# One-hot products of the expert gates: rounded operands in two passes, and one-hots built four tokens at a time

## What is computed

```python
best_s, best_c = lax.top_k(cand_s.reshape(T, PEER_HEADS, K * K), K)
expert_id = jnp.take_along_axis(cand_id.reshape(T, PEER_HEADS, K * K), best_c, axis=-1)
gate = jax.nn.softmax(best_s, axis=-1)
...
u = expert_down[ib]
a = jnp.einsum('pd,ped->pe', xb, u).astype(jnp.float32)
act = jax.nn.gelu(a, approximate=False) * gb
v = expert_up[ib]
return jnp.einsum('pe,ped->pd', act.astype(xb.dtype), v)
```

## Time and profile before

| what | value |
|---|---|
| median of 3 runs | 1441.38 us (1441.08 to 1443.99) |
| the profiled execution | 1449.68 us |
| its span | 1447.7 us |
| TensorE matmuls busy | 1318.6 us, 91% |
| VectorE busy | 984.3 us, 68% |
| ScalarE busy | 663.0 us, 46% |
| GpSimd busy | 288.2 us, 20% |
| mean granted TensorE clock | 0.954 |

### The profile page before, as it was taken

One profiled execution on the slowest core, in us unless ns is written; L12 is line 12 of the kernel. 1 busy time (PEld: TensorE's weight loads), 2 busy tenths in 40 slices (PEclk: granted clock), 3 DMA queues, 4 the chain that ended last, 5 costly groups with the idle time before them and its releaser, 6 DMA issues.

```text
span 1447.7 us, 20176 instructions
## 1 busy us (share of the span) xinstructions
PE 1318.6 (91%) x8170; PEld 1166.8 (81%) x8170; DVE 984.3 (68%) x1888; ACT 663.0 (46%) x863; POOL 288.2 (20%) x166
## 2 busy tenths in 40 slices
PE   3687987999999999999999999999979993799998
PEld 2575846899999999999888888888856783689987
DVE  5879745699999989844677677667655553455554
ACT  1445323355555554444544545445433733345443
POOL 0005000018876886750000000000000023000000
PEclk7788999999999999999999999999989996999999
DMA  9763535787787778887987887887526231335542
GB/s 346 261 233 124 177 116 180 256 295 219 230 257 238 220 218 255 260 277 290 329 285 284 302 277 278 313 274 269 211 89 228 91 87 59 116 117 201 205 176 88
DMA packets 144791, 316.11 MB, mean 218 GB/s; under 512 B 26286, under 2 KB 72623, under 8 KB 139322
## 3 DMA queue, kind: packets, MB, share of 16 engines
q1 hardware_dynamic: 105754, 263.35, 51.2%
q0 software_dynamic: 24928, 17.91, 6.6%
q10 hardware_dynamic: 14016, 33.56, 6.2%
HBM read 279.06 MB, written 34.67 MB: 217 GB/s over the span
## 4 chain that ended last, share of the span: by engine, by line
PE 75%; DVE 14%; DMA 5%; ACT 2%; POOL 1%; issue 1%; SPq 1%; POOLq 0%; DVEq 0%; ACTq 0%
PE ps L635 10%; PE ps L634 10%; PE ps L636 10%; PE ps L622 9%; PE ps L623 9%; PE ps L624 9%; PE ps L612 3%; PE ps L614 3%; PE ps L613 3%; DVE w_lo L1482 3%; DVE peer_arena L1845 2%; DVE peer_arena L1844 2%; DMA pages<-arena 2%; DMA arena<-in_ada_w 2%; PE ps L681 1%
## 5 line engine op out<-in xcount | busy, mean ns | idle before, releaser
L1482 DVE TENSOR_TENSOR w_lo<-wring,w_hi 128x1024 fp32r<-128x1024 f32 (+1 forms) x404 | 489.0, 1218 | 250.5 <-ACT w_hi L1076 247.7
L1076 ACT CAST w_hi<-wring 128x1024 fp32r<-128x1024 f32 (+1 forms) x404 | 420.2, 1045 | 361.0 <-PE ps L624 227.3
L622 PE MATMUL ps<-hT_hi,w_hi 128*128 128x256 f32 x1408 | 395.6, 281 | 14.4 <-DVE hT_lo L1505 5.3
L623 PE MATMUL ps<-hT_lo,w_hi 128*128 128x256 f32 x1408 | 393.5, 279 | 0.0
L624 PE MATMUL ps<-hT_hi,w_lo 128*128 128x256 f32 x1408 | 393.3, 279 | 0.0
L622 PEld LDWEIGHTS ps<-hT_hi,w_hi 128*128 128x128 f32 x1408 | 267.5, 190 | 16.3 <-DVE hT_lo L1505 5.5
L624 PEld LDWEIGHTS ps<-hT_hi,w_lo 128*128 128x128 f32 x1408 | 267.8, 190 | 0.0
L1431 POOL DMA_INDIRECT gates_of_second<-late x128 | 238.2, 1861 | 145.4 <-DVEq L1780 58.2
L623 PEld LDWEIGHTS ps<-hT_lo,w_hi 128*128 128x128 f32 x1408 | 266.7, 189 | 0.3
L635 PE MATMUL ps<-w_lo,a_hi 128*128 128x512 f32 x640 | 251.9, 394 | 0.0
L634 PE MATMUL ps<-w_hi,a_hi 128*128 128x512 f32 x640 | 250.4, 391 | 0.0
(11 more groups left out here) (293 smaller groups left out, 1278.7 us busy)
## 6 DMA issues: line engine op xcount, KB each, us to landing
wring<-in_peer_down SPq DMA_DIRECT2D x32, 2048.0 KB
wring<-in_peer_up SPq DMA_DIRECT2D x32, 2048.0 KB
wring<-in_w_in SPq DMA_DIRECT2D x12, 2048.0 KB
pages<-in_ada_w POOLq DMA_DIRECT2D x8, 2048.0 KB, 8.5
acts_by_expert<-pages ACTq DMA_DIRECT2D x32, 512.0 KB, 3.9
peer_arena<-acts_by_expert SPq DMA_DIRECT2D x32, 512.0 KB, 8.6
wring<-in_w_up SPq DMA_DIRECT2D x8, 2048.0 KB
wring<-in_w_down SPq DMA_DIRECT2D x8, 2048.0 KB
```

Source lines behind the costliest of these rows:

```text
L622: pe.matmul(o, hi[:, k, :], hT_hi[:, k, :], start=(k == 0), stop=False)
L623: pe.matmul(o, hi[:, k, :], hT_lo[:, k, :], start=False, stop=False)
L1076: act.copy(split_part(kind, w_hi, u, width(kind, j)), part_of(kind, wring[:, n % RING, :], u, width(kind, j))).then_inc(split_hi, 1)
L1482: dve.tensor_tensor(lo, part_of(kind, wring[:, n % RING, :], u, width(kind, j)), hi, ALU.subtract)\
```

## The change

The one-hots and the gate become float32r. The gate is divided into a rounded part `gateT_hi` and the rest `gateT_lo`, as the weights are. A batch's one-hots are in three layers: first keys, second keys times the rounded gate, second keys times the rest, and each token has two float32r products that add up in PSUM in place of one float32 product. VectorE makes the one-hots of both keys for four tokens in one comparison of two tensors (128 x 1024), waits for it, and multiplies the second keys' layer (128 x 512) by the two parts of the gate. `onehot` has its own tensor of 12288 numbers a partition, at the address of `peer_arena`. Nothing else changes.

```diff
+            with ExitStack() as onehot_only:
+                onehot = onehot_only.enter_context(nc.sbuf_tensor("onehot", [P, OB, 3, OT, NKEY], F32R))
...
-                        mm = pe.matmul(psf[:, at:at + NKEY], onehot[:, q % OB, 1, t, :], onehot[:, q % OB, 0, t, :],
-                                       start=True, stop=True)
+                        pe.matmul(psf[:, at:at + NKEY], onehot[:, q % OB, 1, t, :], onehot[:, q % OB, 0, t, :],
+                                  start=True, stop=False)
+                        mm = pe.matmul(psf[:, at:at + NKEY], onehot[:, q % OB, 2, t, :], onehot[:, q % OB, 0, t, :],
+                                       start=False, stop=True)
                     mm.then_inc(S["onehot_used"], 1)
...
-            own(dve.tensor_copy(selT.rearrange("p k t -> p (k t)"), ps[:, 4, 0:3 * P]))
+            dve.tensor_copy(selT.rearrange("p k t -> p (k t)"), ps[:, 4, 0:2 * P])
+            own(dve.tensor_copy(gateT_hi[:, :], ps[:, 4, 2 * P:3 * P]))
+            own(dve.tensor_tensor(gateT_lo, ps[:, 4, 2 * P:3 * P], gateT_hi[:, :], ALU.subtract))
...
-                for t in range(OT):
-                    at = q * OT + t
-                    first, second, weight = (selT[:, k, at:at + 1] for k in range(3))
-                    dve.tensor_scalar(onehot[:, q % OB, 0, t, :], con("iota"), first, None, ALU.is_equal)
-                    ins = dve.tensor_scalar(onehot[:, q % OB, 1, t, :], con("iota"), second, weight, ALU.is_equal, ALU.mult)
-                ins.then_inc(S["onehot_ready"], 1)
+                tokens = slice(q * OT, (q + 1) * OT)
+                numbers = con("iota").unsqueeze(1).unsqueeze(1).to_broadcast([P, 2, OT, NKEY])
+                own(dve.tensor_tensor(onehot[:, q % OB, 0:2], numbers,
+                                      selT[:, :, tokens].unsqueeze(3).to_broadcast([P, 2, OT, NKEY]), ALU.is_equal))
+                dve.tensor_tensor(onehot[:, q % OB, 2], onehot[:, q % OB, 1],
+                                  gateT_lo[:, tokens].unsqueeze(2).to_broadcast([P, OT, NKEY]), ALU.mult)
+                dve.tensor_tensor(onehot[:, q % OB, 1], onehot[:, q % OB, 1],
+                                  gateT_hi[:, tokens].unsqueeze(2).to_broadcast([P, OT, NKEY]), ALU.mult)\
+                    .then_inc(S["onehot_ready"], 1)
```

More of the change, by code:

```diff
@@ L246, in two_blocks @@
         st = sb("st", [P, 10, 16])
+        gateT_hi = sb("gateT_hi", [P, P], F32R)
         cbias = sb("cbias", [P, 2, 2])
@@ L303, in two_blocks @@
         qryT = peer_arena[:, 0:16 * T].rearrange("p (c t) -> p c t", c=16)
-        onehot = peer_arena[:, 0:8192].rearrange("p (s k t n) -> p s k t n", k=2, s=OB, t=OT)
         score = peer_arena[:, 4096:8192].rearrange("p (b h n) -> p b h n", b=NB, h=PH)
@@ L323, in two_blocks @@
         chosen = late[:, 384:896].rearrange("p (k b h n) -> p k b h n", k=2, b=NB, h=PH)
-        selT = late[:, 896:1280].rearrange("p (k t) -> p k t", k=3)
+        selT = late[:, 896:1152].rearrange("p (k t) -> p k t", k=2)
+        gateT_lo = late[:, 1152:1280]
         gates_first = nc.dram_tensor("gates_of_first", (P // 16, P, NKEY * 16), F32, kind="Internal").ap()
```

## The result

The changed kernel takes 1459.48 us (median of 4 runs, 1457.67 to 1461.61), the kernel before beside it 1442.49 us (4 runs, 1441.08 to 1443.99). The medians are 17.0 us apart, a ratio of 1.0118. The ratio on record, which is not exactly that of the medians, is 1.0109 with a 95% interval of 1.0093 to 1.0126, or 13.4 to 18.2 us. The prediction had 1458.6 us.

What follows compares the result with a forecast made beforehand. VectorE, not TensorE, was taken to bound the stage; its splits end 18.0 us later, less 0.8 saved on TensorE's last turn, so 1441.4 + 17.2 = 1458.6 us, range 1453 to 1467.

Steps and rivals of the forecast that it cites:

- The bound: In the stage of the change, VectorE and not TensorE sets the end: 4.935 us a turn against 4.52.
- VectorE's turn of 6.06 us: On VectorE, a split of 1.14 us and two batches of 2.46 us make a turn, against 4.935 before.
- 18.0 us for the splits: On VectorE, the split of part 95 comes at 621.1 in place of 603.13, 18.0 us later.
- The saving is only worth something at the last turn, 1.70 - 0.91 = 0.8 us.: On TensorE, cheaper products at 0.057 us each gain 0.8 us once, since TensorE is not waited for earlier.
- The Trainium skill's 81 ns: On TensorE, a 128-column matmul in a stream with weight loads takes about 81 ns, making a turn's products 1.3 us.
- TensorE's idle time: In the stage, TensorE waits about 2.2 to 2.4 us a turn for VectorE's split, with a busy share near 65%.
- The sum: Over the whole kernel, 18.0 us lost on VectorE less 0.8 saved on TensorE: 17.2 us slower.
- Dear products: Rival: narrow float32r products on TensorE cost 0.213 us each, so TensorE bounds the stage, 24 us later, 1465.5; chance 0.12.
- The clock: Rival: TensorE, 60% busy in the stage, falls to 1.2 GHz, giving 1462 to 1480 us; chance 0.05. Forecast itself expected 1.00.
- No change: Rival: VectorE was not the stage's bound, TensorE's slack takes up the loss, and time stays 1441; chance 0.03.
- faster: Rival: VectorE's batched instructions run at the one-source rate, a turn is 3.9 us, 13 us earlier, 1428; chance 0.04.
- The quicker pace behind the stage: If idle time kept parts 2.72 us apart, not 2.83, for 32 parts behind the stage, 3.5 us return: 1455.

Runs made afterwards that it cites:

- both thin kernels: The changed kernel and the kernel before, each with one batch of one-hots behind each of 32 parts, not two behind each of 16: 1440.09 and 1441.27 us.

## Why the prediction was right, and where not

- **The bound.** Right. The chain, in order of time, is VectorE up to 616.75, and two kernels that take half of TensorE's products away, at either length of VectorE's turn, gained 1.3 and 1.0 us.
- **VectorE's turn of 6.06 us.** Right to the hundredth: 6.06 over 15 turns, from rows of unlike lines (a chained pair, an unchained pair, a split). The comparison with its wait measured 1.25 against 1.26, the multiplications 0.61 against 0.60. That the loss is the doubled numbers at a two-source price, and not the batching, is shown: batched without the rest of the gate, the turn is 4.86.
- **18.0 us for the splits.** Right. From the first split to that of part 95 it is 616.67 - 519.68 = 96.99 us, against 603.13 - 524.04 = 79.09 before, which is 17.9; the stage grew by 18.0.
- **"The saving is only worth something at the last turn, 1.70 - 0.91 = 0.8 us."** The mechanism is right, the price is not. This is the term that was wrong: a product of 128 columns was priced at 0.057, half of one of 256, because price was taken to go by the columns that pass. It measured 0.111, set by the load of 128 new stationary columns, and 16 of them take 1.73 us. The term is 0, not 0.8. The prediction's argument that nothing in the rows ties a price to more than the columns that pass and the type falls with it. The rows of before left it open: 0.11 us between matmuls of 256 columns might be the pass or the load, and the float32 instructions of 128 columns at 0.106 hinted that it was not the pass.
- **The Trainium skill's 81 ns** (TensorE: Matmul & The Clock Gate, Back-to-back issue gap) for such a stream was not borne out. 111 ns were measured. The same page's rule for the load, an estimate of 107 ns, comes nearer.
- **TensorE's idle time.** Predicted at 2.2 to 2.4 us a turn, measured 1.2 to 1.4 ahead of ten parts and none shown ahead of the others, because the products cost 0.8 us more and the parts at the lower clock fill the rest. The predicted 2.2 us appeared in the kernel without the second pass. The busy share, predicted near 65%, was 80 to 87% from 540 to 600 us, for the same two reasons.
- **The sum.** 17.2 us predicted, 17.0 between the medians, 18.0 in the stage's own trace. That 17.2 lies so close to 17.0 is luck: the sum without the wrong term is 18.0, and the interval of 13.4 to 18.2 us can't tell the two apart. What confirms the sum is the distance of the splits, not the median.
- **Dear products.** The prices considered were 0.057 and 0.213 us. The measured 0.111 is between, below the 0.20 from which it decides.
- **The clock.** The forecast's sign of a clock of 1.00 was wrong. It fell three times, as the rival had it, and came back once TensorE was full, as the rival had it. The rival charged up to half of 40 us for it, and it cost nothing: it fell for most of one part at a time and never for a whole turn, and such a turn needs 4.4 + 1.7 = 6.1 us, about VectorE's 6.06. That used up the margin. A part at 1.2 GHz throughout would take 24 x 0.213 = 5.1 us, an estimate from the distance of its matmuls (551.98 to 552.62 for three), and with 1.7 for the products more than VectorE's turn; no run shows one.
- **No change; faster.** Both fell: the batched instructions took 1217 and 693 ns, the two-source price, and the chain was read rightly.
- **The quicker pace behind the stage.** The casts are 2.72 us apart in the profiled execution, as in the prediction's lower case, against 2.83 before. But idle time in the stage is not what it takes: both thin kernels had none and still the quick pace behind it.

## What to carry to other kernels

Before making work cheaper on the busiest engine, walk the chain of waits through that stage in order of time: here TensorE was 91% busy and half its products were worth 1 us, because in this one stage VectorE had 0.4 us more to do in each turn. When side work rides along a stream of parts, first choose how densely: one batch a part in place of two took away the whole loss and made a saving on TensorE worth 14 to 17 us that had been worth 1. Price a vector instruction by numbers times its rate (float32 with two sources cost 1.05 ns a number here, with one 0.55) and only then by count, and a narrow float32r product with a new stationary operand by the columns loaded (0.11 us for 128, though only 64 or 128 move).

## What the runs showed of the hardware

- A float32r product costs 0.111 us from start to start with 128 new stationary columns, whether 64 or 128 columns move, 0.113 with 256 moving, and 0.06 with 64 stationary and 128 moving ones.
- TensorE's granted clock fell to 1.2 GHz (0.50 from 552 to 553 us) in a stage in which it was never idle for more than some 1.4 us at a time, once in 6 us at most, and rose again within 4 us (551.37 to 555.09).
- At a granted clock of 1.00 the 256-column matmuls run at one of two paces, 0.113 or 0.118 us, for tens of microseconds at a time: behind the stage in the kernel before and in the one with batched float32 one-hots, and from 520 to 530 us in the changed one. Over 100 us the slow pace would cost 4 us, an estimate from 0.118 against 0.113. Its cause stays open; no run was made to find it.
